# x also read transposed from DRAM; projections on unnormalised x, the row factor applied behind them

## The reference

```python
def _rms_norm(x, gain):
    y = x32 * lax.rsqrt(jnp.mean(x32 * x32, axis=-1, keepdims=True) + EPS)
    return (y * gain)
...
h = _rms_norm(x, norm_mix[l])
proj = h @ w_in[l]
q, k, v, cb, cc, cu = jnp.split(proj, splits, axis=-1)
q = _rms_norm(q.reshape(b, s, N_ATTN_HEADS, HEAD_DIM), q_norm[l])
k = _rms_norm(k.reshape(b, s, N_ATTN_HEADS, HEAD_DIM), k_norm[l])
attn = _stick_breaking_attention(q, k, v)      # A[t,s] = sigmoid(z_ts) * prod (1 - sigmoid(z_tj)), s < t
conv = _short_conv_mixer(cb, cc, cu, conv_w[l]) # B * conv3(C * u)
x = x + jnp.concatenate([attn, conv], -1) @ w_out[l]
```

## Time and profile before

| | us |
|---|---|
| median of 3 runs (lowest, highest) | 2436.81 (2435.79, 2438.77) |
| profiled execution, its own time | 2439.77 |
| span in the profile, first to last instruction | 2438.0 |
| opening ends, attention begins (first unit's scores) | 305.94 |
| last matmul of attention (a.v, line 1388) | 982.34 |

### The profile page before, as it was taken

The page is one execution under the profiler, slowest core; times in us unless marked ns, Lnnn a source line. Parts: engine busy times, 40 slices in busy tenths (PEclk is TensorE's granted clock), DMA queues, the critical chain, the costliest instruction groups (busy, mean ns, idle before and its releaser), DMA issues.

```text
span 2438.0 us, 33295 instructions
## 1 busy us (share of the span) xinstructions
PE 2405.6 (99%) x11880; PEld 2015.0 (83%) x11880; DVE 1456.5 (60%) x1499; ACT 1165.8 (48%) x1866; POOL 1240.2 (51%) x880
## 2 busy tenths in 40 slices
PE   8999999999999999999999999999999999999999
PEld 6888878888888888888888888888878888888887
DVE  4444377787777777436755555556645555554555
ACT  4322277788777777323533333334533333333333
POOL 1455367878787877104754544306755545440021
PEclk9999999999999999999999999999999999999999
DMA  6989874443634641534333233386743232325665
GB/s 199 312 286 289 253 222 108 143 113 101 176 84 120 175 132 54 172 130 165 124 112 125 78 116 110 124 291 224 230 150 110 88 125 78 116 95 193 223 218 199
DMA packets 337503, 388.07 MB, mean 159 GB/s; under 512 B 21472, under 2 KB 242784, under 8 KB 335072
## 3 DMA queue, kind: packets, MB, share of 16 engines
q1 hardware_dynamic: 337376, 386.49, 50.3%
HBM read 263.20 MB, written 123.21 MB: 158 GB/s over the span
## 4 chain that ended last, share of the span: by engine, by line
PE 90%; DVE 2%; DMA 2%; SPq 2%; issue 2%; ACT 1%; POOL 1%; ACTq 0%; DVEq 0%; POOLq 0%
PE lay_ps L2582 11%; PE lay_ps L2584 11%; PE lay_ps L2586 11%; PE lay_ps L106 8%; PE lay_ps L107 8%; PE lay_ps L108 8%; PE lay_ps L2612 5%; PE lay_ps L2613 5%; PE lay_ps L2614 5%; PE lay_ps L1381 5%; PE lay_ps L1369 2%; PE lay_ps L1388 2%; PE lay_ps L1368 2%; PE lay_ps L1387 2%; POOL lay_A L2486 1%
## 5 line engine op out<-in xcount | busy, mean ns | idle before, releaser
L2486 POOL TENSOR_TENSOR lay_A<-lay_raw,lay_A 128x512 fp32r<-128x512 f32 x264 | 365.0, 1395 | 376.1 <-ACT lay_A L2101 375.9
L2582 PE MATMUL lay_ps<-lay_B,lay_A 128*128 128x512 f32 x1232 | 479.6, 389 | 0.4 <-DVE lay_B_over L1741 0.2
L2584 PE MATMUL lay_ps<-lay_B,lay_A 128*128 128x512 f32 x1232 | 479.3, 389 | 0.0
L2586 PE MATMUL lay_ps<-lay_B,lay_A 128*128 128x512 f32 x1232 | 479.3, 389 | 0.0
L1288 POOL TENSOR_TENSOR lay_a<-lay_a,lay_stick 128x128 f32<-128x128 f32 (+5 forms) x192 | 282.4, 1478 | 105.1 <-DVE lay_stick L1229 48.3
L2351 DVE TENSOR_TENSOR lay_A<-lay_A_over,lay_A 128x1024 fp32r<-128x1024 f32 x154 | 215.9, 1403 | 163.9 <-ACT lay_A L2145 163.5
L2101 ACT ACTIVATE lay_A<-lay_raw 128x512 fp32r<-128x512 f32 x264 | 162.0, 627 | 282.9 <-DMA lay_raw<-in_w_gate 110.2
L2145 ACT ACTIVATE lay_A<-lay_A_over 128x1024 fp32r<-128x1024 f32 x154 | 163.1, 1060 | 242.5 <-PE lay_ps L2614 214.5
L2582 PEld LDWEIGHTS lay_ps<-lay_B,lay_A 128*128 128x128 f32 x1232 | 231.3, 188 | 49.3 <-POOL lay_A L2486 1.0
L2586 PEld LDWEIGHTS lay_ps<-lay_B,lay_A 128*128 128x128 f32 x1232 | 231.3, 188 | 47.9
L2584 PEld LDWEIGHTS lay_ps<-lay_B,lay_A 128*128 128x128 f32 x1232 | 231.3, 188 | 47.8
(11 more groups left out here) (145 smaller groups left out, 4979.5 us busy)
## 6 DMA issues: line engine op xcount, KB each, us to landing
hid_ops<-lay_s SPq DMA_DIRECT2D x154, 256.0 KB, 2.0
lay_A_over<-hid_ops SPq DMA_DIRECT2D x154, 256.0 KB, 2.8
lay_w_stage<-in_w_in SPq DMA_DIRECT2D x48, 512.0 KB, 4.8
lay_raw<-in_w_gate SPq DMA_DIRECT2D x22, 1024.0 KB, 5.6
lay_raw<-in_w_up SPq DMA_DIRECT2D x22, 1024.0 KB, 8.1
lay_A_over<-wd_ops SPq DMA_DIRECT2D x88, 256.0 KB, 3.0
lay_A_over<-in_w_down SPq DMA_DIRECT2D x66, 256.0 KB, 4.6
lay_wd_raw<-in_w_down SPq DMA_DIRECT2D x11, 1024.0 KB, 6.8
```

Source lines behind the costliest of these rows:

```text
L2486: nc.gpsimd.tensor_tensor(A[:, j, p, 1, :, :], operand(j, p), A[:, j, p, 0, :, :].bitcast(F32), ALU.subtract).then_inc(lo_done, 1)
L2582: nc.tensor.matmul(ps[:, b, :], A[:, j, p, 0, k, :], B[p][:, 0, k, :], start=first_mm, stop=False, skip_group_check=True)
L2584: nc.tensor.matmul(ps[:, b, :], A[:, j, p, 0, k, :], B[p][:, 1, k, :], start=False, stop=False, skip_group_check=True)
L2586: mm = nc.tensor.matmul(ps[:, b, :], A[:, j, p, 1, k, :], B[p][:, 0, k, :], start=False, stop=last_mm, skip_group_check=True)
```

## The change

x is given to the kernel in two more layouts, made on the host: `x_columns` is x transposed, and `x_tiles` has each tile of 128 rows as the transposed blocks that the opening uses. The gain comes as eight columns of 128.

In the opening the tile of x^T is loaded from `x_tiles`, multiplied by the gain on VectorE (`gain_part`) and split in SBUF. The projections work on this unnormalised product. The row factor is applied behind: to v in the two halves of its split, and for q and k, whose own norm cancels it, only through the eps, which is multiplied by the mean square of the row (`eps_x`). The squares are still summed from the row layout x. The 128 transposes of x, the normalising of x on VectorE and the stores of h^T are gone; x is loaded twice (once in each layout), and the 128 row factors of each tile are stored to DRAM (`row_rstd`). The loops are written out.

For the convolution's projections a block of x^T (128 values by 512 rows) is loaded into one of six buffers `raw`, GpSimd multiplies it by the row factors (`norm_row`), ScalarE rounds it times the gain (`row_hi`) and VectorE takes the rest (`row_lo`), 8 blocks for each pair, 32 in all. Which unit does which is in the four tables `ROW_LOADS` to `ROW_LO` (a number of NU = 48 or more is a unit of the pair itself). For pair 0, blocks 0 to 5 are loaded in tile 6, multiplied in tiles 7 to 12 and split in tile 15. `COUNT` of pairs 1 to 3 moves one step of the first projection from unit 4 to unit 2 and one to unit 3, and one of a late projection from unit 43 to unit 42.

```diff
+            load_xT(0)
+            load_w_third(0)
+            sp.dma_start(gain[:, :], gain_cols).then_inc(gain_in, DMA)
+            load_w_third(1)
+            load_xT(1)
+            load_w_third(2)
+            for k in range(1, KT):
...
+                    load_x(0)
+                if k == 3:
+                    load_xT(2)
+                if k == 4:
+                    load_x(1)
                 if k >= 2:
                     sp.wait_ge(w_lo_done, w_count(k - 2))
                 sp.dma_start(w_stage[:, k % 2, :], w_in[k * P:(k + 1) * P, 0:COLS]).then_inc(w_in_sem[k % 2], DMA)
...
+                sp.wait_ge(qkT_lo_done, 2 * t + 2)
...
+            def step(t, b):
+                if t + 2 < TILES:
+                    load_x(t + 2)
+                    if t >= 2:
+                        load_xT(t + 2)
...
+                if t == EARLY_ROWS:
+                    att.load_early_rows(sp)
...
+                if t == TILES - 1:
+                    att.load_rows(sp)
+                    store_r(t)
+                    store_qk(t - 1)
+                    store_v(t)
+                    return
+                store_r(t)
+                if t > 0:
+                    store_qk(t - 1)
+                store_v(t)
...
+            def step(t, b):
+                if 2 <= t + 1 < TILES:
+                    x_rstd(t + 1)
+                if t - 1 - FIRST_PIECE in range(PIECES):
                     piece(t - 1 - FIRST_PIECE)
+                if t - EARLY_ROWS - 1 in range(RAW):
+                    att.norm_row(pool, t - EARLY_ROWS - 1)
                 pool.wait_ge(qk_ss_done, t + 1)
-                nc.gpsimd.tensor_tensor(qk_msq[:, :], qk_ss[:, :], cst["eps"][:, 0:2 * HEADS],
+                pool.wait_ge(eps_done, t + 1)
+                nc.gpsimd.tensor_tensor(qk_msq[:, :], qk_ss[:, :], eps_x[:, b:b + 1].to_broadcast([P, 2 * HEADS]),
...
+                if 3 <= t < TILES - 1:
+                    for n in range(NB):
+                        hT_part(t + 1, n)
...
+                if t == TILES - 1:
+                    qkT_part(t - 1, 0)
+                    for i in range(RAW):
+                        att.hi_row(act, i)
...
+                head_square(t, 1)
+                qkT_part(t - 1, 1)
+                if t > 2:
+                    v_part(t)
...
+            def gain_part(t, n):
+                dve.wait_ge(xT_in[t % 2], DMA * (t // 2 + 1))
+                part = xT[:, t % 2, 4 * n:4 * n + 4, :]
+                nc.vector.tensor_tensor(part, part, gain[:, 4 * n:4 * n + 4].unsqueeze(2).to_broadcast([P, 4, P]),
+                                        ALU.mult).then_inc(xg_done, 1)
+            def hT_part(t, n):
                 dve.wait_ge(hT_hi_done, NB * t + n + 1)
-                nc.vector.tensor_tensor(hT_lo[:, b, 4 * n:4 * n + 4, :], x_bank(t, n),
-                                        hT_hi[:, b, 4 * n:4 * n + 4, :].bitcast(F32),
+                nc.vector.tensor_tensor(hT_lo[:, t % 2, 4 * n:4 * n + 4, :], xT[:, t % 2, 4 * n:4 * n + 4, :],
+                                        hT_hi[:, t % 2, 4 * n:4 * n + 4, :].bitcast(F32),
                                         ALU.subtract).then_inc(hT_lo_done, 1)
...
+                nc.vector.scalar_tensor_tensor(out=v_out[:, t % 2, :, HD:2 * HD],
+                                               in0=proj[:, t % 2, 2, 0:AD].rearrange("p (h d) -> p h d", d=HD),
+                                               scalar=rstd[:, t % 2:t % 2 + 1],
+                                               in1=v_out[:, t % 2, :, 0:HD].bitcast(F32),
+                                               op0=ALU.mult, op1=ALU.subtract).then_inc(v_done, 1)
...
-            def x_transpose(t, b, n):
-                pe.wait_ge(xn_done, t + 1)
-                wait(pe, hT_lo_done, NB * (t - 1) + n + 1 if early(t) else NB * t + n)
-                if not opened(t):
-                    pe.wait_ge(qkT_lo_done, 2 * (t - 2))
-                for j in range(4):
-                    k = 4 * n + j
-                    last = nc.tensor.transpose(x_bank(t, n)[:, j, :], xn[:, b, k * P:(k + 1) * P], cst["ident"][:, :])
-                last.then_inc(tx_full, 1)
...
+            def begin(k, t):
+                if k > 0 and t == 0:
+                    pe.wait_ge(w_lo_done, w_count(k))
+                if k % 4 == 0:
+                    pe.wait_ge(hT_lo_done, NB * t + k // 4 + 1)
+                for n in range(3):
+                    if k == 0 and t == 0:
+                        pe.wait_ge(w_lo_done, n + 1)
+                    last = matmul3(nc, proj[:, t, n, 0:AD], hT_hi[:, t, k, :], hT_lo[:, t, k, :],
+                                   w_hi[:, n, k, :], w_lo[:, n, k, :],
+                                   k == 0, k == KT - 1)
+                    if k == KT - 1:
+                        last.then_inc(proj_full, 1)
+            for k in range(KT - 2):
+                for t in range(2):
+                    begin(k, t)
             for t in range(2):
...
-    COUNT = [2, 1, 0, 3, 2, 5, 1, 1, 1, 2, 2, 2, 2, 1, 1, 3, 2, 1, 3, 1, 4, 5, 1, 2,
-             2, 0, 1, 1, 4, 3, 3, 0, 2, 2, 1, 3, 2, 1, 2, 4, 1, 4, 1, 3, 3, 4, 1, 0]
+    COUNT = [2, 1, 1, 4, 0, 5, 1, 1, 1, 2, 2, 2, 2, 1, 1, 3, 2, 1, 3, 1, 4, 5, 1, 2,
+             2, 0, 1, 1, 4, 3, 3, 0, 2, 2, 1, 3, 2, 1, 2, 4, 1, 4, 2, 2, 3, 4, 1, 0]
...
+    ROW_LOADS = {8: [0], 9: [1], 10: [2], 16: [3], 17: [4], 18: [5], NU - 2: [6, 7]}
+    ROW_NORM = {18: [0], 19: [1], 22: [2], 26: [3], 28: [4], 30: [5], NU - 1: [6, 7]}
+    ROW_HI = {NU - 3: [0, 1], NU - 1: [2, 3], NU: [4], NU + 1: [5, 6], NU + 2: [7]}
+    ROW_LO = {NU - 1: [0, 1], NU: [2, 3], NU + 1: [4], NU + 2: [5, 6, 7]}
+    def row_steps(table, p, n):
+        ahead = [(p + 1, i) for i in table.get(n, ())] if p < PAIRS - 1 else []
+        return ([(p, i) for i in table.get(n + NU, ())] if p > 0 else []) + ahead
...
+            def load_r(p):
+                wait(sp, row_normed, KT * p)
+                if p == 0:
+                    for b in range(2):
+                        sp.wait_ge(opening.r_stored[b], DMA * (BANK // P // 2))
+                if p == 1:
+                    for b in range(2):
+                        sp.wait_ge(opening.r_stored[b], DMA * (TILES // 2))
+                sp.dma_start(r_row[:, :], r_dram[p * BANK:(p + 1) * BANK].partition_broadcast(P)).then_inc(r_in, DMA)
+            def load_raw(p, i):
+                n = KT * p + i
+                wait(sp, row_done, n - RAW + 1)
+                sp.dma_start(raw[:, n % RAW, :], xT[i * P:(i + 1) * P, p * BANK:(p + 1) * BANK]).then_inc(raw_in[n % RAW], DMA)
...
+            def load_early_rows(sp):
+                load_r(0)
+                for i in range(RAW):
+                    load_raw(0, i)
             def load_rows(sp):
-                sp.wait_ge(opening.proj_full, 3 * (TILES - 1) + 1)
-                for i in range(KT):
-                    load_hT(0, i)
-                    if i == 1:
-                        load_w(0, 2)
+                for i in range(RAW, KT):
+                    load_raw(0, i)
+                load_w(0, 2)
...
+                        if n == 12:
+                            load_r(p + 1)
+                        for i in ROW_LOADS.get(n, ()):
+                            load_raw(p + 1, i)
...
+            def row_hi(p, i):
+                act.wait_ge(row_normed, KT * p + i + 1)
+                if is_first(p):
+                    act.wait_ge(opening.proj_full, 3 * (TILES - 1) + 1)
+                elif i < KT - 1:
+                    act.wait_ge(hT_used, (KT - 1) * (p - 1) + i + 1)
+                else:
+                    act.wait_ge(proj_full, NPROJ * p)
+                nc.scalar.activation(hT_hi[:, i, :], raw[:, (KT * p + i) % RAW, :], ACT.Copy,
+                                     scale=gain[:, i:i + 1]).then_inc(row_hi_done, 1)
...
+            def row_lo(p, i):
+                dve.wait_ge(row_hi_done, KT * p + i + 1)
+                nc.vector.scalar_tensor_tensor(out=hT_lo[:, i, :], in0=raw[:, (KT * p + i) % RAW, :],
+                                               scalar=gain[:, i:i + 1], in1=hT_hi[:, i, :].bitcast(F32),
+                                               op0=ALU.mult, op1=ALU.subtract).then_inc(row_done, 1)
...
+            def norm_row(p, i):
+                n = KT * p + i
+                if i == 0:
+                    pool.wait_ge(r_in, DMA * p + DMA)
+                pool.wait_ge(raw_in[n % RAW], DMA * (n // RAW) + DMA)
+                nc.gpsimd.tensor_tensor(raw[:, n % RAW, :], raw[:, n % RAW, :], r_row[:, :],
+                                        ALU.mult).then_inc(row_normed, 1)
...
-                    pe.wait_ge(hT_in[i], 2 * DMA * p + 2 * DMA)
+                    pe.wait_ge(row_done, KT * p + i + 1)
...
+    nc = bacc.Bacc("TRN2", target_bir_lowering=False, num_devices=1,
+                   dynamic_dma_scratch_size=SCRATCH)
+    x, gain = inputs["x"][0], inputs["norm_mix"][0]
```

(4 more changed lines are left out.)

572 lines of the change are left out of this document (248 added, 324 removed).

## The result

| | before | after |
|---|---|---|
| median of 4 runs (lowest, highest), us | 2437.05 (2435.79, 2438.77) | 2496.40 (2493.40, 2500.23) |
| ratio to before, 95% interval | | 1.0244 [1.0226, 1.0262] |
| span of the profiled execution, us | 2438.0 | 2498.4 |

A forecast was written before the change was run, and what follows sets the result against it. TensorE, busy for 99% of the span, was taken to bound the kernel. 2439.8 - 10.4 - 3.4 - 2.2 - 5.4 + 10.8 = 2429.2, less 3.0 from profiled to median scale, gave 2426 us; range 2414 to 2443.

The forecast's parts named there:

- The opening's loop: Opening, 12 tiles: the transposes of x go from TensorE, which nothing covers; -10.4 us.
- the start: Up to the third tile: first matmul earlier, but the weights' last split bounds; third tile at 46.5, not 49.96; -3.4 us.
- tiles 2 and 3: Opening, 49.96 to 70.35 us: TensorE's 20.4 us fall to 18.1 without x's transposes and the wait for x; -2.2 us.
- Into attention: Opening to attention: TensorE's waits for h^T (1.8) and v (1.9) and the lowered clock (1.7) go; -5.4 us.
- The pair ends: Ends of pairs 0 to 2: making h^T there, with rests waiting for GpSimd, costs +3.6 us each, +10.8 together.
- Rival 3: Pair ends: rests and GpSimd alternate, TensorE waits, clock falls; 10.7 us each, 2447 us, slower; chance 0.18.
- Rival 2: Gains eaten by boundaries of 6 to 8 us, opening's gain multiplications or v's wait; 2432 to 2441 us; chance 0.19.
- Rival 1: Pair ends are free: VectorE's work fits and TensorE is three units ahead; 1.2 us each, 2419 us; chance 0.26.
- the prediction's middle value: Pair ends: each rest takes 0.68 us plus 0.54 waiting, on average, for half a GpSimd instruction.

The follow-up runs named there:

- one: The changed kernel, wait kept, with each tile's store of row factors replaced by one 512-byte row copied from x in DRAM (wrong factors): 2441.8 us.
- r16: The changed kernel with a column of row factors for each of 16 tiles, so GpSimd no longer waits for the factors' store: 2457.4 us, ratio 1.0085.
- r16_norm: r16 with GpSimd's products of rows for pairs 1 to 3 cut to 8 of 512 columns: 2447.8 us.
- r_late: The changed kernel with 16 columns, no wait, and the factors of tiles 4 to 15 stored in pair 0; everything computed: 2443.9 us, ratio 1.0026.
- r16_two: r16 with each tile's 128 row factors stored twice, to two places in DRAM: 2473.0 us.
- spread2: The kernel before, with h^T normalised on chip from loaded x^T, factors spread by TensorE, no row work in attention, start mended: 2434.3 us, ratio 0.9990.
- r_first: The changed kernel, wait and two columns kept, with the row factors' store issued first in its tile, ahead of the loads and the piece's store: 2483.6 us.
- r16_lo: r16 with VectorE's rests of rows for pairs 1 to 3 cut to 8 of 512 columns: 2446.3 us.

## Why the prediction was wrong

**The step that failed** is the sentence under the sum: "The two row layouts cost nothing else on the path: the factor's store is 128 numbers a tile". It priced a store by its bytes, and the wait on `r_stored` that the change adds on GpSimd was not seen. What the runs show in its place: the store lands after 14.4 us, closes a loop of 20 to 25 us a tile through SyncE's queue, and costs 55 us (`after` less `one`), more than all other terms. Some 39 of them go with the wait (`r16`), the others are the small pieces in the queue. No row of the kernel before shows a store of four-byte pieces, so this had to be bounded from both sides, and was not.

**The opening's loop, the start and tiles 2 and 3: right once that is out.** Forecast -10.4 - 3.4 - 2.2 = -16.0 to the first scores; `one` has 289.6 against 305.9, -16.4. Term by term it is -9.7, -4.4 and -2.3: its third tile starts at 45.6 us (49.96 before) and what stood at 70.35 before now at 63.7.

**Into attention: right.** Forecast -5.4; `one` has +1.4 up to the first running product (4.4 against 3.0) and -6.3 in pair 0 up to its unit 44, -4.9 in all. (The whole of pair 0 has only -4.6, because the first row work stands in its last unit.) TensorE's waits for h^T and for v are gone from it.

**The pair ends: right mechanism in part, mis-sized.** Forecast +3.6 each; `one` has +7.0, +7.3 and +9.0 from unit 44 to unit 44. The rests took 1.30 each in `after`, the forecast's 0.68 + 0.54 nearly. What it had wrong is what a delay in the chain is worth: it took VectorE's idle time as free, but moved to the middle of the pair, with rests at 0.73 and a quarter of slack on each engine, the same work cost 8 us too. The products on GpSimd, put at 1.09 each and at nothing in the middle and 0.7 at the end, take 1.29 each and carry a third (2.9, 2.4 and 2.1 in `r16_norm`). The moved steps of COUNT, put at a gain of 1.4, cost 1.2 without row work, but beside it they seem to gain 1.2, so that term was near.

**The sum without the store:** -16.4 - 4.9 + 23.3 = +2.0, and `one`'s span is 2440.0 against 2438.0. So even without the failed step the forecast of -11 would have been off, by the pair ends. **Rival 3** named the place (8.8 at each boundary, a fallen clock) and had the size of `after`, 8.9, 8.7 and 8.8. But it was not what made the kernel 59 us slower, and that its side, slower, came true is luck. **Rival 2** (2432 to 2441) is nearly what `one` (2441.8) and `r_late` (2443.9) come to. **Rival 1** is refuted.

The Trainium skill, page "SBUF — State Buffer", section "Who interferes with whom", says that a VectorE instruction with two SBUF inputs and a GpSimd instruction that reads SBUF exclude each other. The row of 8 columns above agrees: 2.41 us beside one of 2.39. The rests' own time came out near the prediction's middle value (1.30 for 1.22), the boundary's didn't.

What stays open: how GpSimd's product, ScalarE's round and VectorE's rest share the 6 to 8 us in the middle of a pair; why the third boundary costs 9.0 in `one` (8.8 in `r_late`), 1 to 2 more than the first two; and how the four-byte writes delay the other transfers (they queue with them or hold the memory), which no view here tells apart.

## What to carry to other kernels

Price a transfer by its number of pieces and by what stands behind it in its queue, not by its bytes, and ask for each semaphore that a change adds which loop it closes: SyncE issues in order, so a wait for one small store ties an engine to everything issued ahead of it. Idle time of an engine in a chained loop is no cover: the row work cost some 8 us a pair where each engine had a quarter of its time idle, and putting one of its steps behind the instruction that TensorE awaits gave back only 1.0 to 2.4. And let one experiment take the suspected transfer's form away rather than its wait: the wait's removal gave 39 us and looked like the cause, the form's gave 55 with the wait in place.

## What the runs showed of the hardware

- 128 writes of 4 bytes from 128 partitions landed after 14.4 us in a full queue (`after`), a row of 512 bytes copied out of DRAM in the same place after 7.1 (`one`); the 512 KB store behind it took 12.9 and 3.4 us. A second such store in each tile cost about 1.0 us a tile (`r16_two`).
- While such writes drained (`r_late`, 312 to 321 us), the DMA engines were busy for 0.935 and moved 86 GB/s; the same engines moved 340 GB/s at 1.04 in `spread2`.
- In front of a full queue SyncE took up to 9.03 us to issue one store of 512 KB (`r_first`), and 0.58 in `one`.
- A VectorE instruction with two operands in SBUF waited for a whole GpSimd instruction even with 8 columns: 2.41 us, where two of them took 0.34 together (`r16_lo`).
